# Two transformer blocks in fp32 on one core: first groups behind four norms on rows not yet normalised

## The reference

```
def rmsnorm(x, g):
    y = x * lax.rsqrt(jnp.mean(x * x, axis=-1, keepdims=True) + EPS)
    return y * g

# first block, layers 0 and 1
h = rmsnorm(x, norm_mix_pre[l]);  proj = h @ w_in[l]
(q, k, v, g_ret, sc_b, sc_c, sc_x, cf_a, cf_b, gate_logits) = split(proj)
o = head_groupnorm(retention(rotary(q), rotary(k), v))
glu = cf_a * sigmoid(cf_b);  c = silu(layernorm(causal_dwconv(glu, 31 taps)))
x = x + rmsnorm(merged @ w_o[l], norm_mix_post[l])
h = rmsnorm(x, norm_ffn_pre[l]);  up = causal_dwconv(h @ w_up[l], 3 taps)
x = x + rmsnorm((silu(gate) * val) @ w_down[l], norm_ffn_post[l])

# second block, layers 2 and 3
xn = rms(x, norm_mix_g);   z = xn @ w_in_2   # mLSTM, sparse and differential attention
x = x + merged @ w_out
xn = rms(x, norm_ffn_g);   g, u = split(xn @ w_gate_up)
x = x + (silu(g) * u) @ w_down
```

## Time and profile before

| | |
|---|---|
| median of 3 runs | 1834.47 us (1834.27 to 1837.68) |
| span of the profiled execution | 1830.6 us (the profile lists no other time of it) |
| TensorE busy | 1777.5 us, 97% |
| VectorE busy | 1360.9 us, 74% |
| ScalarE busy | 1073.6 us, 59% |
| GpSimd busy | 191.1 us, 10% |
| mean granted TensorE clock | 1.000 |

### The profile page before, as it was taken

One profiled execution on the slowest core, in us unless ns is written; L12 is line 12 of the kernel. 1 busy time (PEld: TensorE's weight loads), 2 busy tenths in 40 slices (PEclk: granted clock), 3 DMA queues, 4 the chain that ended last, 5 costly groups with the idle time before them and its releaser, 6 DMA issues.

```text
span 1830.6 us, 36315 instructions
## 1 busy us (share of the span) xinstructions
PE 1777.5 (97%) x14784; PEld 1731.1 (95%) x14784; DVE 1360.9 (74%) x2385; ACT 1073.6 (59%) x1808; POOL 191.1 (10%) x200
## 2 busy tenths in 40 slices
PE   8999999999999999999999989999999998999998
PEld 8999999999999999999999879999999998899998
DVE  6898789867889779876768868655557697686553
ACT  5455666655455657654776576544458757755442
POOL 1002410001002410001201003000002100020000
PEclk9999999999999999999999999999999999999999
DMA  7545546564645536664645634556545564346563
GB/s 282 175 158 185 182 138 201 194 207 143 204 160 180 184 128 209 194 206 140 193 150 169 203 104 143 180 196 196 194 151 184 161 200 130 107 168 197 196 195 105
DMA packets 90341, 320.06 MB, mean 175 GB/s; under 512 B 10528, under 2 KB 12992, under 8 KB 90048
## 3 DMA queue, kind: packets, MB, share of 16 engines
q1 hardware_dynamic: 90176, 317.75, 53.7%
HBM read 310.60 MB, written 1.08 MB: 170 GB/s over the span
## 4 chain that ended last, share of the span: by engine, by line
PE 74%; DVE 15%; ACT 5%; issue 3%; POOL 1%; DMA 1%; SPq 0%; DVEq 0%; ACTq 0%; POOLq 0%
PE big L589 68%; PE small L589 4%; DVE L L1113 4%; DVE POOL L1470 4%; ACT H L1889 1%; PE small L588 1%; DVE POOL L1302 1%; DVE POOL L1668 1%; POOL POOL L2485 1%; ACT POOL L2311 1%; ACT POOL L2273 1%; ACT L1985 0%; POOL POOL L2464 0%; DVE FL L1280 0%; DVE POOL L1309 0%
## 5 line engine op out<-in xcount | busy, mean ns | idle before, releaser
L589 PE MATMUL big<-HH,H 128*128 128x256 f32 x3344 | 940.1, 281 | 5.3 <-ACT HH L1922 3.3
L589 PE MATMUL big<-HL,H 128*128 128x256 f32 x3344 | 925.2, 277 | 3.9 <-DVE HL L1248 3.8
L589 PE MATMUL big<-HH,L 128*128 128x256 f32 x3344 | 924.3, 276 | 0.0
L1113 DVE TENSOR_TENSOR L<-F,H 128x1024 fp32r<-128x1024 f32 x574 | 703.8, 1235 | 203.0 <-ACT H L1889 201.7
L1889 ACT ACTIVATE H<-F 128x1024 fp32r<-128x1024 f32 x582 | 610.7, 1055 | 205.7 <-PE big L589 202.8
L589 PEld LDWEIGHTS big<-HH,H 128*128 128x128 f32 x3344 | 628.2, 188 | 10.7 <-issue 5.5
L589 PEld LDWEIGHTS big<-HL,H 128*128 128x128 f32 x3344 | 628.4, 188 | 7.5 <-DVE HL L1248 5.7
L589 PEld LDWEIGHTS big<-HH,L 128*128 128x128 f32 x3344 | 627.9, 188 | 0.0
L589 PE MATMUL big<-FH,H 128*128 128x256 f32 x848 | 238.5, 281 | 0.0
L589 PE MATMUL big<-FH,L 128*128 128x256 f32 x848 | 234.4, 276 | 0.0
L589 PE MATMUL big<-FL,H 128*128 128x256 f32 x848 | 234.4, 276 | 0.0
(11 more groups left out here) (237 smaller groups left out, 1797.4 us busy)
## 6 DMA issues: line engine op xcount, KB each, us to landing
F<-in_stream SPq DMA_DIRECT2D x582, 512.0 KB, 4.0
POOL<-POOL SPq DMA_DIRECT2D x32, 128.0 KB, 3.9
POOL<-head_rows SPq DMA_DIRECT2D x8, 256.0 KB, 5.1
X<-in_x SPq DMA_DIRECT2D x2, 512.0 KB, 4.8
POOL<-POOL SPq DMA_DIRECT2D x16, 64.0 KB, 3.0
out_x<-X SPq DMA_DIRECT2D x1, 1024.0 KB, 3.9
POOL<-in_decay SPq DMA_DIRECT2D x1, 768.0 KB, 11.1
POOL<-POOL SPq DMA_DIRECT2D x8, 96.0 KB, 5.7
```

Of the source, the lines that this page charges most:

```text
L589: return pe.e.matmul(out_, lhsT, rhs, start=start, stop=stop)
L1113: v.tensor_tensor(L[:, j % NR, :], F[:, j % NF, :], H[:, j % NR, :].bitcast(F32), ALU.subtract).then_inc(s_lo, 1)
```

## The change

Four norms, b = 0, 5, 6 and 7, get a number of raw groups, 5, 1, 2 and 1 (`RAW`). Those groups do not take normalised rows: ScalarE rounds X times gain (`high_raw`), VectorE makes the low part of it (`low_raw`), row by row as X becomes final, and the factor is multiplied in afterwards. For a channel group VectorE multiplies the PSUM result by S, the factor spread over the partitions, into one of four SBUF tiles RAWT (`scaled_out`), and whoever read the bank before reads that tile; the bank is free when the tile is written. For the token group `m_v` the factor is the scale of ScalarE's copy. The normalised rows are still made, from S, which ScalarE copies from PSUM to SBUF: within the norm for b = 5 and 7, and in pairs beside the groups behind the first one for b = 0 and 6. The first group of such a norm runs in another order inside a row (all high products, all low products of x, all low products of the weights), and the column sums of the last row and the product that spreads the factor stand between its rows. The spare products of these norms go. For b = 5 and 7 the sum of squares takes in row 6 on VectorE, which it did not before. At the start SP first issues the eight gain columns and piece 0, then x; four of the squares of x go to GpSimd. Code for raw groups behind the summed norms comes along, but no such norm is in RAW.

```diff
+RAW = {0: 5, 5: 1, 6: 2, 7: 1}
+        S = tile(22)
+        RAWT = sb("RAWT", [P, 4 * T])
-            return 5 if b % 2 else 6
+            return 5 if b % 2 and b not in RAW else 6
 # TensorE
+                if before is not None and before.raw and before.kind != "t":
+                    pe.wait_ge(raw_v.sem, raw_v.at(*before.raw))
+            def raw_blocks(g):
+                b, n = g.raw, len(g.members)
+                banks_ = [bank_for(m)[:, 0:T] for m in g.members]
+                for k in range(KT):
...
+                    wait_x(m, k, False)
+                    for ps, (j, hi, lo) in zip(banks_, places):
+                        pe.wait_ge(s_hi, j + 1)
+                        mm(ps, hi, xh, start=(k == 0), stop=False)
+                    wait_x(m, k, True)
+                    for ps, (j, hi, lo) in zip(banks_, places):
+                        mm(ps, hi, xl, start=False, stop=False)
+                    for i, (ps, (j, hi, lo)) in enumerate(zip(banks_, places)):
+                        pe.wait_ge(s_lo, j + 1)
+                        r = mm(ps, lo, xh, start=False, stop=(k == KT - 1))
...
+                    beside_row(b, k)
+            def beside_row(b, k):
...
+                if k == (6 if b == 0 else 0):
+                    if b == 0:
+                        bank = use(0, b, "yy")
+                        pe.wait_ge(bnd_v.sem, bnd_v.at(b, "add", 0, 7))
+                        wide_sums(bank, (0, 1), tile(YSQ), True, True).then_inc(s_fill[0], 1)
+                    else:
+                        sums_of(b, 7, False, True)
+                if k == (7 if b == 0 else 2):
+                    pe.wait_ge(bnd_v.sem, bnd_v.at(b, "dg"))
+                    mm(use(2, b, "s1")[:, 0:T], ones, tile(DG)).then_inc(s_fill[2], 1)
 # VectorE
+            def low_raw(b, k):
+                dve.wait_ge(rh_a.sem, rh_a.at(b, k))
+                v.scalar_tensor_tensor(out=raw_low(b, k), in0=X[:, k, :], scalar=par(gain, l, k),
+                                       in1=raw_high(b, k).bitcast(F32), op0=ALU.mult, op1=ALU.subtract)
+            def raw_norm(b):
+                if b == 0:
+                    low_parts(1)
+                    low_raw(b, 0)
+                    low_raw(b, 1)
+                    low_parts(2)
...
+                    for i in range(4, KT):
+                        first_squares(i)
+                    low_parts(5)
+                    v.tensor_copy(kept(b), sums_in(bank))
+                else:
+                    low_parts(first + AHEAD)
+                v.reciprocal(col(4, 2), col(2, 2))
+                diagonals(col(4, 2), tile(DG), bnd_v, b, "dg")
+                if b:
+                    low_raw(b, 7)
+                    low_parts(first + AHEAD + 1)
+                if b % 2:
+                    for pair in range(4):
+                        normal_rows(b, pair)
+                        if pair == 2:
+                            low_parts(first + AHEAD + 2)
+            def scaled_out(m):
+                was_read(b, "s2" if b in SUMMED else "s1")
+                dve.wait_ge(s_mm, m.done)
+                v.tensor_tensor(landed(m), big[m.banks[0]][:, 0:T], S, ALU.mult)
 # VectorE, behind the sum of `out` j or `down` j into X
+                if b in RAW and b not in SUMMED and j < 7:
+                    low_raw(b, j)
 # VectorE, in each group behind the first of b = 0 and 6
+                for pair in pairs:
+                    normal_rows(g.raw, pair)
 # ScalarE, behind the square of row j
+                    if b in RAW:
+                        high_raw(b, j)
 # GpSimd
+                if b == 0 and b in RAW:
+                    for i in range(4, KT):
+                        q.tensor_tensor(tile(YSQ + i), X[:, i, :], X[:, i, :], ALU.mult)
 # SP
+            q.dma_start(PR[:, c:c + KT], params[:, c:c + KT]).then_inc(s_gain, 16)
+            pieces(0, 1)
             q.dma_start(X[:, 0:4, :], xT[:, 0:4, :]).then_inc(s_x, 16)
+            pieces(1, 3)
             q.dma_start(X[:, 4:8, :], xT[:, 4:8, :]).then_inc(s_x2, 16)
             q.dma_start(CO[:, 0:256], consts[:, 0:256]).then_inc(s_ones, 16)
-            pieces(0, 2)
-            q.dma_start(PR[:, :], params).then_inc(s_par, 16)
-            pieces(2, NF)
+            pieces(3, 4)
+            q.dma_start(PR[:, c + KT:], params[:, c + KT:]).then_inc(s_par, 16)
+            pieces(4, NF)
```

More of the change, by code:

```diff
@@ L190, in __init__ @@
         self.banks, self.done, self.act, self.dve = [], 0, 0, 0
+        self.raw = None
 class Group:
@@ L492, in norm_dve @@
         def norm_dve(b):
+            if b == 0 and b in RAW:
+                return [(b, "add", 0, i) for i in range(1, KT)] + [(b, e) for e in ("kept", "r", "dg")] + \
+                    [(b, "full", n) for n in range(KT)]
             if b == 0:
@@ L533, in fresh, with first_of, is_landed, landed @@
             return G[n].named("out") or G[n].named("down"), None
+        def first_of(b):
+            return [n for n in range(len(G)) if fresh(n) == (True, b)][0]
+        for b, groups in RAW.items():
+            i = 0
+            for g in G[first_of(b):first_of(b) + groups]:
+                g.raw = b
+                for m in g.members:
+                    m.raw, i = (b, i), i + 1
+        raw_v = tally("raw_scaled", [m.raw for b in sorted(RAW) for g in G if g.raw == b for m in g.members
+                                     if m.kind != "t"])
+        def is_landed(lane, m):
+            if m.raw and m.kind != "t":
+                lane.wait_ge(raw_v.sem, raw_v.at(*m.raw))
+            else:
+                lane.wait_ge(s_mm, m.done)
+        def landed(m):
+            return RAWT[:, m.raw[1] % 4 * T:(m.raw[1] % 4 + 1) * T] if m.raw else big[m.banks[0]][:, 0:T]
+        def pairs_in(n):
+            b = G[n].raw
+            if b is None or b % 2 or n == first_of(b):
+                return []
+            i, per = n - first_of(b) - 1, 4 // (RAW[b] - 1)
+            return list(range(i * per, (i + 1) * per))
         def at_norm(n):
@@ L1082, in tensor_program @@
                     beside.finish(name)
-                for _ in token_blocks(g) if g.kind == "t" else channel_blocks(g):
+                blocks = token_blocks if g.kind == "t" else raw_blocks if g.raw is not None and b is not None else channel_blocks
+                for _ in blocks(g):
                     if not made_after:
@@ new lines, in normal_rows @@
+            def normal_rows(b, pair):
+                layer, e = use_of(b)
+                gain, l = gain_of(b)
+                was_read(b, "s2" if b in SUMMED else "s1")
+                dve.wait_ge(s_par, 16)
+                for n in (2 * pair, 2 * pair + 1):
+                    v.scalar_tensor_tensor(out=normal(b, n), in0=X[:, n, :], scalar=par(gain, l, n), in1=S,
+                                           op0=ALU.mult, op1=ALU.mult).then_inc(bnd_v.sem, bnd_v.up(b, "full", n))
+                low_x(b, 2 * pair)
@@ new lines, in scaled_out @@
+            def scaled_out(m):
+                b, i = m.raw
+                was_read(b, "s2" if b in SUMMED else "s1")
+                if i >= 4:
+                    before = [x for g in G if g.raw == b for x in g.members][i - 4]
+                    dve.wait_ge(s_eva, before.act)
+                    dve.wait_ge(s_evd, before.dve)
+                dve.wait_ge(s_mm, m.done)
+                v.tensor_tensor(landed(m), big[m.banks[0]][:, 0:T], S, ALU.mult).then_inc(
+                    raw_v.sem, raw_v.up(b, i))
@@ L1795, in settle @@
             def settle(n, low=0):
-                for m in G[n].members:
-                    if low:
+                for i, m in enumerate(G[n].members):
+                    if m.raw and m.kind != "t":
+                        scaled_out(m)
+                    if low and (i % 2 == 0 or not m.raw):
                         low_parts(low)
@@ L1987, in token_weights @@
             def token_weights(m):
-                act.wait_ge(s_mm, m.done)
-                bank = big[m.banks[0]]
+                is_landed(act, m)
+                bank = landed(m)
                 for e in range(2):
```

327 lines of the change are left out of this document (280 added, 47 removed).

## The result

The changed kernel takes 1850.2 us, median of 4 runs (1849.6 to 1854.7); the kernel before took 1834.4 beside it (4 runs, 1832.5 to 1837.7). The ratio is 1.0093, with a 95% interval of 1.0074 to 1.0112. The forecast was 1834.0 with a range up to 1840: wrong, and on the wrong side. The profiled executions lie 1849.0 - 1830.6 = 18.4 us apart by their spans, and two things are in the difference: norms that cost more, and the clock. The mean granted clock of TensorE is 0.992 after and 1.000 before.

What follows compares the result with a forecast made beforehand. TensorE, busy 97% of the span, was taken as the bound, with norms where its products go unread. Terms 3.7 - 2.4 - 1.8 = -0.5, with 3.9 carried over from span to median, gave 1834.0; own range 1830 to 1837, full range 1822.5 to 1840.

Steps and rivals of the forecast that it cites:

- the sum said -0.5: All norms: 3.7 at b = 0, -2.4 at b = 6, -1.8 for b = 5 and 7 together, giving -0.5 us.
- The third rival: First groups: spare products go, TensorE stands still 2 us, clock falls; 2.9 a norm, +8.2 in all, 1842.7; chance 0.03.
- what lies around: Whole kernel: the median shown, 1834.47, lies 3.9 us above the profiled span 1830.6; carried over whole.
- b = 5 and 7: -0.9 forecast: Norms ahead of the FFNs of layers 2 and 3: 2.3 gained, 0.9 and 0.5 given back; -0.9 us each.
- the first group starts at about 1159.3: Norm b = 5: sum of out 7 at 1158.7, first group at about 1159.3; 2.3 us gained against 1161.55.
- semaphore, 0.4 and semaphore: End of a raw group: VectorE scales each bank before it is free, some 0.5 us that was not there.
- the second rival: VectorE beside GpSimd: contention stretches low pieces and eight normal rows, 0.33 more each; +4.9, 1839.4; chance 0.17.
- b = 6: -2.4 forecast: Norm ahead of layer 3: first group 4.4 us earlier, net 3.0 after costs, 0.6 of it lost; -2.4 us.
- 0.6 of the 3.0 as lost: Behind norm b = 6: VectorE comes out of the second group about level, so later TensorE waits take 0.6 us.
- b = 0: +3.7 forecast: The start: VectorE's twelfth low piece 3.7 us late, TensorE's lead lost at 77.14, TensorE then 3.7 later.
- everything behind is a chain: Layer 0 behind the twelfth low piece: its 3.7 us lateness passes through the query turn to TensorE's wait at 77.14.
- Rival 1 (a lead kept): Start: VectorE catches up before 77 us, TensorE's lead stays, -3.5; 1826.8, or 1822.2 with a free out loop; chance 0.35.

Runs made afterwards that it cites:

- the profile with the clock held in norms 1, 2, 5 and 7: Changed kernel plus 14 spare products ahead of TensorE's wait in norms b = 5 and 7; median 1851.1 us, this profiled run 1843.9.
- The load run: Kernel before plus 12 useless VectorE operations of 256 columns at the start, TensorE untouched; 1837.7 us, ratio 1.0010.
- the run without spare products at its norms: Kernel before with the spare products taken out of norms b = 5, 6 and 7, no raw groups; 1842.0 us, ratio 1.0033.
- the late-rounding kernel: Kernel before with raw groups at b = 5 and 7 only, raw rounding of member j-1 behind the sum of member j; 1833.9 us, ratio 0.9986.
- the filled start: Kernel with raw rows at norm 0 alone, plus 20 spare products in TensorE's waits between 35 and 43 us; 1845.4 us, ratio 1.0048.
- the sized products: Kernel before with its spare products sized to the idle times of its own trace; 1832.0 us, ratio 0.9979.

## Why the prediction was wrong

Take the profile with the clock held in norms 1, 2, 5 and 7 (span 1842.2) as the measure of the terms: 11.6 us over before, where the sum said -0.5. Another 6.8 us, nearly all of it clock, lie between it and after.

1. **The clock was priced in the wrong place and given 0.03.** The third rival had the mechanism: the spare products go, TensorE stands still ahead of the first groups, the clock falls. Against it stood one row, 1.90 us of idle at 77.14 followed by full spacing. One case without a fall was read as a rule. The load run has the same wait (2.1 us) and a fallen clock behind it; so has the run without spare products at its norms. It fell behind this wait in three of the nine profiles with the old start, and not in the others. The price of 2.9 a norm was too high: 1.4 to 2.4 measured. But the places were too few: the profile of after also shows it at two norms that the change leaves alone. There it varies from run to run: the kernel before has it too, in its median run for some 4 us, but not in the run that was profiled, whose clock is 1.000. The forecast took the one execution's clock as the kernel's. It also carried 3.9 us over whole as "what lies around" the span; in the later runs, of all kernels, it is 1.7 to 3.4 us, mostly 1.7, and the rest was that the profiled execution was a quick one.

2. **b = 5 and 7: -0.9 forecast, +1.5 measured at full clock.** Two steps failed. The first is "the first group starts at about 1159.3". In after, less the offset of 8.1, the last sum comes at 1159.3, where 1158.7 was forecast. Behind it stand four products of column sums (1167.57, 0.64 us), and the first product of the group, at 1168.21, comes at 1160.1. So 1.3 us are gained at the start of the group and not 2.3. The two products inside cost 0.8, as forecast (0.9). The second step is the end of the group. It was to cost 0.5, "semaphore, 0.4 and semaphore"; TensorE waited 1.55, and with what lies around the wait it is 1.8. The two make 2.3 of the 2.4 us of the miss. VectorE was at its normal rows when the bank was ready, as this timeline of after shows:

```profile
1178.47 1.36 DVE L1397 SCALAR_TENSOR_TENSOR POOL<-X,PR,POOL 128x256 f32<-128x256 f32 x2
1179.75 0.41 DVE L1519 TENSOR_TENSOR HL<-POOL,HH 128x256 fp32r<-128x256 f32 x1
1180.09 1.21 DVE L1254 TENSOR_TENSOR L<-F,H 128x1024 fp32r<-128x1024 f32 x1
1181.22 1.35 DVE L1397 SCALAR_TENSOR_TENSOR POOL<-X,PR,POOL 128x256 f32<-128x256 f32 x2
1182.66 0.42 DVE L1519 TENSOR_TENSOR HL<-POOL,HH 128x256 fp32r<-128x256 f32 x1
1183.00 0.75 DVE L1410 TENSOR_TENSOR RAWT<-big,POOL 128x256 f32<-128x256 f32 x2
```

   Two normal rows that take 0.88 us alone take 1.36 with GpSimd's low row beside them: one of each pair is 0.97 in place of 0.48. The scaling of 1183.00 is queued behind the fourth pair, and TensorE's last product ended at about 1181.9. That is the second rival's mechanism. It cost 1.4 us of VectorE's time in three pairs, where the rival had eight rows of 0.33, but it was set to keep 0.2 a norm; it kept more, since the rows ran past the group's end. By an estimate from these rows VectorE would have been free at 1181.6 without it, in time for the bank; no run takes the contention away. The contention rule of the Trainium skill (GPSIMD Engine Reference, Specifications) that the prediction weighed agrees with these rows. The wait is there at the same length in the late-rounding kernel, which still gains 1.3: moving the rounding out of the loop is worth about 2.8 us a norm against the changed kernel.

3. **b = 6: -2.4 forecast, +3.8 measured, 1.7 of it a fallen clock.** The gain of the early start was near: at its end the group stands 3.1 us early (4.4 less 0.9 forecast). "0.6 of the 3.0 as lost" failed: TensorE waited 0.6 for the scaling, 1.1 for a low piece and 2.0 for ScalarE's scaling of m_v's banks (L2321), which stands in ScalarE's queue behind a small chain of layer 3 (L2553 to L2557). The chain takes 3.9 us, 2.6 of them two ACT_TABLE_LOAD of 1.28 us each, and it stood ahead of this scaling in the kernel before too. But less the offset of 11.1 the scaling begins 3.6 us later than there (1385.57 for 1370.87): ahead of the chain ScalarE now rounds the eight normal rows, and waits 3.0 us in all for VectorE to multiply them. Where TensorE runs ahead, these engines don't: I counted VectorE's work and left ScalarE's out. The wait for ScalarE is read from the trace; it was not taken away in an experiment. In six of the seven profiles with these groups the clock fell once behind them, here or near 1410; the seventh has 16 spare products there. A part of the 5.9 us that the ratios give for this norm (4.9 by the profiles) stays without a row.

4. **b = 0: +3.7 forecast, +4.2 measured: near, and that is luck.** VectorE's twelfth low piece was 5.1 late and not 3.7. Of that the transfer of the queries gave back 1.5, since it took 4.3 us and not 5.9; the forecast took 5.9 as fixed ("everything behind is a chain"), and which of the two comes isn't settled by when it is issued. The other profiles with raw rows at the start have +4.7 to +5.4, and +7.2 where the transfer was long. TensorE's lead was gone by 39 us, between the rows of the first normal group, not at 77; so the wait on the decayed scores shrank to 0.96 and did not grow to 7. That the result hangs on VectorE's chain all the same, the filled start showed: 1.9 us less of lateness on TensorE at 50 us brought nothing.

5. **The frame.** Rival 1 (a lead kept) had 0.35 of the chances and none of its terms appeared. Each of the four norms came out on the costly side of its term, and clock aside for reasons of one kind: a group that starts early is worth only what VectorE and ScalarE can follow, and the change put more work on both at the very place where they had just lost their cover.

## What to carry to other kernels

A product that nobody reads can be worth more than the idle time that it fills: count it as holding the clock, size it to the gap in the trace and put it ahead of the wait. Compare the mean granted clock of all runs, not of the profiled one, before a term of a few microseconds is read from a trace, and look at what stands behind a fallen stretch: where TensorE waits next in any case, it costs nothing. When a TensorE stage is started earlier, list what each other engine owes at the end of that stage; and new work in a loop of sum, square and piece belongs behind the step that the next turn waits for.

## What the runs showed of the hardware

- The granted clock also fell to its lower level behind several short waits in a row, where no single one was longer than about 1 us. In the late-rounding kernel the norm b = 1 has TensorE busy for 2.43 us between 246 and 250, and this window behind it; with the sized products TensorE is busy from 245 to 250 throughout, and the clock stays at 1.00. The profiled run of the kernel before has the same short waits (0.80, 0.61 and 0.95 us) and keeps 1.00, so such waits bring the fall in some executions only.

```profile
250.00:254.00 4.00, 4.00 (x23) 4.00 (x23) 3.96 (x10) 2.09 (x4) 1.79 (x3) 0.57 0.02 4
```

- The same kernel's runs differ by it, though not by it alone: the 22 runs of the kernel before in the first batch go from 1832.2 at clock 0.998 to 1841.3 at 0.994, and at 0.998 they lie between 1832.2 and 1837.0.
- The four 64 KB transfers of the queries took 4.0 to 4.3 us from issue to use in eight profiles and 5.3 to 6.1 in eight, with the same queue of weights around them. Issued at 42.65 they took 4.1, at 43.00 5.9, at 44.47 4.2, at 49.08 4.0 and at 49.28 5.8.
